# Top-16 search of the PEER score vectors moved from the up stage into the query stage of a two-block transformer kernel

## What is computed

```
q = (ht @ peer_wq).reshape(T, 8, 256)
s1 = einsum("thd,hnd->thn", q[..., :128], peer_k1)
s2 = einsum("thd,hnd->thn", q[..., 128:], peer_k2)
v1, i1 = top_k(s1, 16)
v2, i2 = top_k(s2, 16)
cand = (v1[..., :, None] + v2[..., None, :]).reshape(T, 8, 256)
sc, pos = top_k(cand, 16)
experts = take(i1, pos // 16) * 128 + take(i2, pos % 16)
gates = softmax(sc)
```

## Time and profile before

| | us |
|---|---|
| median of 3 runs | 3027.76 (3025.11 to 3029.04) |
| the profiled execution | 3026.6 |
| its span | 3024.8 |
| PE busy, share of the span | 2845.1, 94% |
| DVE busy, share of the span | 2236.1, 74% |
| ACT busy, share of the span | 1481.4, 49% |
| mean granted TensorE clock | 0.973 of 2.4 GHz |

### The profile page before, as it was taken

How to read it: one execution, slowest core, us unless ns; L and a number is a source line. 1 busy time by engine, 2 the same in 40 slices (tenths; PEclk the granted TensorE clock), 3 DMA queues, 4 the chain that set the end, 5 groups by cost and what they waited for, 6 DMA issues and landing times.

```text
span 3024.8 us, 37310 instructions
## 1 busy us (share of the span) xinstructions
PE 2845.1 (94%) x13639; PEld 2369.9 (78%) x13639; DVE 2236.1 (74%) x3019; ACT 1481.4 (49%) x1990; POOL 598.8 (20%) x480
## 2 busy tenths in 40 slices
PE   5979987999999989999999998898999999999998
PEld 3657756888888758776777788898999987888887
DVE  6465547888888853797954329999997867888886
ACT  3443235878888733544452432564665633333332
POOL 0200111111111100000000010033234434444442
PEclk7999988999999999999999998999999999999999
DMA  7544535999999833232333334587789999999995
GB/s 300 169 159 157 198 132 219 362 371 366 362 354 356 305 130 114 96 119 84 105 132 132 129 119 157 180 306 264 273 303 361 337 373 341 365 367 360 362 362 187
DMA packets 203628, 746.30 MB, mean 247 GB/s; under 512 B 24752, under 2 KB 78128, under 8 KB 146352
## 3 DMA queue, kind: packets, MB, share of 16 engines
q1 hardware_dynamic: 124656, 497.12, 45.8%
q0 software_dynamic: 56912, 179.26, 16.9%
q10 hardware_dynamic: 21872, 67.48, 5.8%
HBM read 670.80 MB, written 98.11 MB: 254 GB/s over the span
## 4 chain that ended last, share of the span: by engine, by line
PE 56%; DVE 18%; issue 5%; ACT 3%; DMA 3%; ACTq 0%; DVEq 0%; POOL 0%; SPq 0%; POOLq 0%
PE PS L550 48%; DVE wlo L1897 3%; DVE oh L2673 2%; DVE hf L2687 2%; DVE hf L2699 1%; PE PS L1151 1%; ACT whi L1227 1%; PE PS L1017 1%; PE PS L1029 1%; PE PS L856 1%; ACT HH L1867 1%; DVE zo L2422 1%; DVE sS L2726 1%; DVE i L2569 1%; DVE wkk L2572 1%
## 5 line engine op out<-in xcount | busy, mean ns | idle before, releaser
L1897 DVE TENSOR_TENSOR wlo<-raw,whi 128x2048 fp32r<-128x2048 f32 x392 | 894.7, 2289 | 351.8 <-ACT whi L1227 313.9
L1227 ACT ACTIVATE whi<-raw 128x2048 fp32r<-128x2048 f32 x392 | 750.9, 1916 | 361.2 <-PE PS L550 305.3
L550 PE MATMUL PS<-HH,whi 128*128 128x512 f32 (+1 forms) x2056 | 792.0, 385 | 47.8 <-DVE wlo L1897 24.0
L550 PE MATMUL PS<-HH,wlo 128*128 128x512 f32 (+1 forms) x2056 | 754.6, 367 | 0.0
L550 PE MATMUL PS<-HL,whi 128*128 128x512 f32 (+1 forms) x2056 | 753.3, 366 | 0.0
L550 PEld LDWEIGHTS PS<-HH,whi 128*128 128x128 f32 x2056 | 392.7, 191 | 108.6 <-DVE wlo L1897 25.4
L550 PEld LDWEIGHTS PS<-HL,whi 128*128 128x128 f32 x2056 | 392.9, 191 | 46.3 <-issue 7.7
L550 PEld LDWEIGHTS PS<-HH,wlo 128*128 128x128 f32 x2056 | 391.8, 191 | 43.1
L550 PE MATMUL PS<-whi,HH 128*128 128x512 f32 (+1 forms) x896 | 352.9, 394 | 15.9 <-DVE HL L2729 10.6
L550 PE MATMUL PS<-whi,HL 128*128 128x512 f32 (+1 forms) x896 | 348.2, 389 | 0.0
L550 PE MATMUL PS<-wlo,HH 128*128 128x512 f32 (+1 forms) x896 | 348.1, 389 | 0.0
(11 more groups left out here) (436 smaller groups left out, 3903.4 us busy)
## 6 DMA issues: line engine op xcount, KB each, us to landing
raw<-in_moe_dram SPq DMA_DIRECT2D x192, 1024.0 KB, 7.4
raw<-in_u_units_dram SPq DMA_DIRECT2D x64, 1024.0 KB
raw<-in_v_units_dram SPq DMA_DIRECT2D x64, 1024.0 KB
raw<-in_w_in_dram SPq DMA_DIRECT2D x44, 1024.0 KB
raw<-in_w_ada_dram SPq DMA_DIRECT2D x24, 1024.0 KB, 22.4
acts_dram<-sS ACTq DMA_DIRECT2D x64, 384.0 KB
gates_dram<-XT ACTq DMA_DIRECT2D x24, 1024.0 KB
sS<-acts_dram SPq DMA_DIRECT2D x42, 384.0 KB
```

The lines of the kernel that those rows point to most:

```text
L550: ins = t.matmul(dst, a, b, start=(first and n == 0), stop=(last and n == 2))
L1227: a.inc(a.e.activation(m.whi[p % HRING][:, :, :], m.raw[RAW_SLOT[load_of(p)]][:, :, :], ACT.Copy), "hi", p)
L1897: v.inc(v.e.tensor_tensor(m.wlo[h][:, :, :], m.raw[RAW_SLOT[load_of(p)]][:, :, :], m.whi[h][:, :, :].bitcast(F32), ALU.subtract), "lo_v", p)
```

## The change

1. **The search moves.** `sc` gets two halves. DVE searches vector k of all four tiles (`found(k)`, one `dve_top16` of four) straight from it in the query stage, into `v16` and `i16`, which now hold all four tiles. ACT's copy of scores k waits for `found(k-2)` in place of the DRAM store.
2. **The DRAM trip goes**: 16 stores and 4 loads on POOL's queue, with their waits, and the `s_scratch` tensor.
3. **One `whi`/`wlo` more ahead.** ACT makes `whi` of up unit 2 before its last score copy and DVE makes `wlo` of it before its last search; ACT and DVE no longer meet the others at "scored" (DVE waits there only before the first choice step).
4. **The table of the up stage.** A tile's choice has 10 steps for 13: the four searches are gone, and the two long pick steps (8200 and 6900 in the old table) are five short ones. `vector` starts at `FOUND_NS` = 13000, the margin falls from 4000 to 2000, and rows are spread evenly (120 in the up stage, 136 in the down stage). Gate steps run at most one a row.
5. Small tensors share buffers to make room, so many buffers lie at other addresses; their sizes are the same.

```diff
-CHOICE_NS = (4900,) * 4 + (1500, 4600, 0, 4600, 0, 8200, 6900, 800, 700)
+CHOICE_NS = (1500, 4600, 4600, 2000, 3400, 3400, 3400, 3400, 800, 700)
...
-LAST_GATE, LAST_ROW, UP_ROWS = 121, 126, 116
+FOUND_NS = 13000
+LAST_GATE, LAST_ROW, UP_ROWS = 119, 124, 120
...
-    tensor, vector = 0, 0
+    tensor, vector = 0, FOUND_NS
...
-        while a < CHOICE_STEPS * NT and vector < tensor + 4000:
+        while a < CHOICE_STEPS * NT and vector < tensor + 2000:
...
-                    self.sc = sb(s3, "sc", [128, 4, 128])
+                    self.sc = sb(s3, "sc", [128, 2, 4, 128])
...
         a.wait_ge("keyed", k)
-        if k:
-            a.wait_ge("score_out", k - 1)
+        if k > 1:
+            a.wait_ge("found", k - 2)
...
+    act_high(a, m, FIRST["u_units"] + HRING - 1)
     score(15)
     a.mark("scored")
-    a.wait_all("scored")
-    a.wait_ge("score_out", 15)
...
-    for n in range(8):
-        dve_low(v, m, FIRST["wq"] + n + HRING - 1)
+
+    def found(k):
+        v.wait_ge("sscore", k)
+        dve_top16(v, [(m.v16[:, i, k, :], m.i16[:, i, k, :], m.sc[:, k % 2, i, :], m.wkk[:, i, :]) for i in range(NT)])
+        v.also("found", k)
+
+    for n in range(4):
+        if n:
+            found(4 * n - 2)
+            found(4 * n - 1)
+        dve_low(v, m, FIRST["wq"] + 2 * n + HRING - 1)
+        dve_low(v, m, FIRST["wq"] + 2 * n + HRING)
+        found(4 * n)
+        found(4 * n + 1)
+    found(14)
+    dve_low(v, m, FIRST["u_units"] + HRING - 1)
+    found(15)
     v.mark("scored")
-    v.wait_all("scored")
-    v.wait_ge("score_out", 15)
...
-    for k in range(16):
-        g.wait_ge("sscore", k)
-        g.dma(e.dma_start(bass.AP(m.sd, 128 * k, [[2048, 128], [128 * 2048, 4], [1, 128]]), m.sc[:, :, :]),
-              "score_out", k)
```

More of the change, by code:

```diff
@@ L186, in peer_schedule @@
             vector += 1150
[L187 to L191, removed]
+        rows = chosen.get(0, n)
+        while 0 in chosen and c * (LAST_ROW - rows) < UP_ROWS * (n - rows) and c < UP_ROWS:
             row[2].append(c)
@@ L337, in __init__ @@
         self.mod = sb(ctx, "mod", [128, 48])
-        self.epst = sb(ctx, "epst", [128, 1])
-        self.eps2 = sb(ctx, "eps2", [128, 1])
-        self.warm = sb(ctx, "warm", [128, 1])
+        few = sb(ctx, "few", [128, 8])
+        self.epst, self.eps2, self.warm, self.ss = (few[:, a:b] for a, b in ((0, 1), (1, 2), (2, 3), (4, 8)))
         self.fn = sb(ctx, "fn", [128, 8])
@@ L2590, in dve_pair_ranks @@
     v.own(3)
-    v.inc(e.tensor_copy(quarter, m.i16[:, 0:8, :]), "pick")
+    v.inc(e.tensor_copy(quarter, m.i16[:, i, 0:8, :]), "pick")
     v.own(3)
@@ L2611, in dve_choice_step @@
     G3 = dst.rearrange("p (h k) -> p h k", h=8)
-    if r < 4:
-        v.wait_ge("scores_in", i)
-        dve_top16(v, [(m.v16[:, k, :], m.i16[:, k, :], m.sN[:, k, :], m.wkk[:, k - 4 * r, :])
-                      for k in range(4 * r, 4 * r + 4)])
-        if r == 3:
-            v.also("sn_free", i)
-    elif r == 4:
+    if r == 0:
+        if step == 0:
+            v.wait_all("scored")
         v.own()
-        v.inc(e.tensor_copy(m.i16f[:, :, :], m.i16[:, :, :]), "pick")
+        v.inc(e.tensor_copy(m.i16f[:, :, :], m.i16[:, i, :, :]), "pick")
@@ L2621, in dve_choice_step @@
         for first, n, width, o in ((0, 4, 16, 0), (4, 12, 4, 64)):
             v.inc(e.tensor_tensor(bass.AP(m.cand, o, [[1024, 128], [N_PAIR, 8], [width, n], [1, width]]),
-                                  bass.AP(m.v16, first, [[256, 128], [32, 8], [1, n], [0, width]]),
-                                  bass.AP(m.v16, 16, [[256, 128], [32, 8], [0, n], [1, width]]), ALU.add), "pick")
-    elif r in (5, 7):
-        h = 2 * (r - 5)
+                                  bass.AP(m.v16, 256 * i + first, [[1024, 128], [32, 8], [1, n], [0, width]]),
@@ new lines, in dve_choice_step @@
+    elif r == 3:
+        dve_pair_ranks(v, m, i)
+    elif r in (4, 5, 6, 7):
+        which, half = divmod(r - 4, 2)
+        ranks = bass.AP(m.wkk, 384 + 64 * half, [[512, 128], [1, 64], [0, 16]]) if which else bass.AP(
+            m.paf, 64 * half, [[128, 128], [1, 64], [0, 16]])
+        v.wait_ge("const5", "io16")
+        v.own()
+        v.inc(e.tensor_tensor(m.EQF, ranks, bass.AP(m.some, 0, [[32, 128], [0, 64], [1, 16]]), ALU.is_equal), "pick")
+        v.own()
+        v.inc(e.tensor_tensor(m.EQ, m.EQ, bass.AP(m.i16f, 128 * half + 16 * which,
+                                                  [[256, 128], [32, 4], [0, 16], [1, 16]]), ALU.mult), "pick")
+        v.own()
+        v.inc(e.tensor_reduce((m.e1, m.e2)[which][:, i, 4 * half:4 * half + 4, :], m.EQ, AX.X, ALU.add), "pick")
+    elif r == 8:
@@ L2653, in dve_choice_step @@
                               ALU.subtract), "gsub", i)
-    elif r == 12:
+    elif r == 9:
         v.wait_ge("gexp5", i)
@@ L3034, in pool_peer @@
     for n in range(128):
-        for step in PEER[n][0]:
-            i, r = choice_of(step)
-            if step == 0 or r == 4 and step + CHOICE_STEPS < NT * CHOICE_STEPS:
-                if step:
-                    g.wait_ge("sn_free", i)
-                    i = choice_of(step + CHOICE_STEPS)[0]
-                g.dma(e.dma_start(m.sN[:, :, :].rearrange("p k n -> p (k n)"),
-                                  m.sd[128 * i:128 * i + 128, :, :].rearrange("t k n -> t (k n)")), "scores_in", i)
         for step in PEER[n][2]:
```

60 lines of the change are left out of this document (22 added, 38 removed).

## The result

The changed kernel takes 2982.68 us (median of 4 runs, 2978.2 to 2987.42); the kernel before took 3026.44 beside it (4 runs, 3023.0 to 3029.04). The ratio is 0.9856, 95% interval 0.9838 to 0.9875. I had forecast 2992 with a range of 2984 to 3006.

A forecast was written before the change was run, and what follows sets the result against it. DVE was taken to bound the first two thirds of the up stage, PE the rest. Up stage 36 us less, query stage, DRAM trip, down stage and addresses 0: 3026.6 becomes 2991, median 2992, range 2984 to 3006.

The forecast's parts named there:

- The search in the query stage: Query stage: 16 searches at 5.34 us cost DVE 85 us, the lag stays inside PE's room; priced at 0.
- DRAM trip, unit 2, unit 3: Start of up stage: the 23.7 us score wait and PE's 9.9 us stop go; both units' `wlo` come in time.
- DVE's chain up to the `wlo` of unit 30: Up stage to row 57: 277 us of DVE work plus 7 of waits after 1811.6, done at 2095.6 us.
- PE starts row 60 there: Up stage: PE starts row 60 at 2095.6, has 334.6 us left, ends at 2430.2 for 2466.0: 36 us less.
- the floor of 624.8: Up stage if PE never waited: 624.8 us against 672.8, so 48 us at most; rival chance 0.07, 2979.
- The down stage ... 0 by the rows: Down stage: four fewer gathered rows worth 0, at most 4 us of PE idleness; its start may move a few us.
- The price of the rows by their bytes: Down stage bound by bytes: four rows, 2.1 MB, take 5.8 us, gain 42 instead of 36; rival 2986, chance 0.08.
- Addresses: Whole kernel: other buffer addresses add or resize no instruction; 0, give or take 3 us.
- The base: Starting time: profiled execution of 3026.6 us becomes 2991; the median of runs lies 1.2 us above it.
- near 2430: End of the up stage: gelu 127 near 2430 us as a sign of being right; later than 2445 wrong.
- the search overruns: Query stage: PE stops from about 5.7 us a search, gain gone at 7.6, 3043 at 8.5; chance 0.03.
- The DVE bound for longer: Up stage: waits at 14 and 7 us more for gate chains, gain 22, time 3005; rival, chance 0.17.

The follow-up runs named there:

- the layout alone: Kernel before with only the change's packing and order of small buffers ahead of the PEER layer: ratio 0.9985 to the kernel before, median 3019.2 us.
- The doubled search: Changed kernel with each of the 16 query-stage searches made twice: 3067.56 us, ratio 1.0144 to the kernel before.
- The run with the late exponential: Changed kernel with ACT's softmax exponential four rows and DVE's finish five rows behind the pick, gate steps starting later: median 2973.78 us, ratio 0.9833.
- the one with slower rows: Late-exponential kernel with gathered rows due at 0.6 a row until the fourth tile's choice is made, faster after: median 2967.94 us, ratio 0.9815.
- the faster version: Changed kernel with late exponential, slower gathered rows and 128 rows gathered in the up stage: median 2964.74 us, ratio 0.9804 to the kernel before.
- with the table: Kernel before with only the change's table rules, 120 rows gathered in the up stage, searches and DRAM trip left in place: ratio 0.9957.
- with the last due rows put back: Changed kernel with LAST_GATE 121 and LAST_ROW 126 for 119 and 124, still 120 rows: median 2983.8 us, ratio 0.9868 to the kernel before.

## Why the prediction was wrong, step by step

- **The search in the query stage: right.** Counted from the last `qT2` copy, which came 9.2 us earlier than in the profile before, the last search should end at 1802.4 us; it ended at 1802.5. ACT's copies wait 9.5 us for searches in seven waits, the longest 3.0, and PE never stops for them; the stage is 0.3 us longer, as it is with the layout alone. One search takes 5.42 us start to start where I had taken 5.34:

```profile
1726.59 0.87 DVE L2573 MAX8 v<-sc 128x8 f32<-128x128 f32 x4 [0.45 <-ACT sc L1755]
...
1732.01 0.88 DVE L2573 MAX8 v<-sc 128x8 f32<-128x128 f32 x4
```

- **DRAM trip, unit 2, unit 3: right.** No wait for scores, no stop for a `wlo`.
- **DVE's chain up to the `wlo` of unit 30: right.** 284 us forecast from the last search, 281.4 measured (1802.5 to 2083.9), with the 28 `wlo`, 41 gate steps and 41 rows that I had counted and 6.4 us of waits, where I had 7 and three of 1.7 for the exponentials. The doubled search confirms that it is one chain.
- **"PE starts row 60 there": wrong, 11.9 us.** This is the step of the up stage that failed. I let PE be held by `wlo` alone, so that it could run ahead of DVE's row 57 by the ring's depth. When that `wlo` was done, at 2083.9, PE had finished only row 58's matmuls and stood in its gate product, and it began row 60 at 2095.8. What held it was ACT's exponential, behind a DVE that came 8.8 us late: 6.3 of the 11.9 us are this stop and 1.3 the slower row 59 after it, and the other 4.3 remain, for which the earlier stops (9.11 and 1.80 us) are the likely cause. I had read that wait the other way only, DVE 1.72 us for ACT, and had allowed 7 us on DVE's side for gate waits where they had to be counted on PE's. From row 60 on the price was good: 332.7 us against 334.6. The shorter chain and these last rows gave back 4.5 us, so the stage missed by 7.4. The run with the late exponential takes back 11.4 us, and the one with slower rows ends at 629.3, near the floor of 624.8 that I had worked out from the earlier trace rows.
- **"The down stage ... 0 by the rows": wrong, 10.6 us, and the miss that put the time below the range.** The miss of the up stage worked the other way. I had read PE's 406 of 410 us from the earlier trace rows, a window that begins 74 us behind the start of the stage, and had written that the start "may move a few us either way" without looking at it. The rows before it show PE at 54.0 us of 60 with a clock of 0.95: 8.7 us lost that could be won, and 5.9 were. Most of the rest are the four gathered rows: 3.3 to 3.8 us in the kernel before (against the layout run and against before), 6.4 for eight in the changed kernel. PE's 4 us of idleness in that window, my "at most", was about what the rows were worth.
- **The price of the rows by their bytes: half right.** My estimate by bytes, from the 362 GB/s of the earlier trace rows, was 5.8 us for four rows, or 1.45 each; the sum took 0, and the runs say 3.8 at most. A row cost 0.83 to 0.95 us between 116 and 120 rows in the kernel before, 0.80 between 112 and 120 in the changed one, and 0.45 between 120 and 128 in the faster version, where PE was busy 399.3 of 400 us. So at a DMA share of 1.00 with PE at 99% neither set the pace alone. The Trainium skill (SBUF - State Buffer, "A bandwidth-pool intuition that's wrong (but worth ruling out)") says that HBM is almost always the end-to-end bottleneck; this stage agrees with it only in part, at 0.45 to 0.95 us a row.
- **Addresses: 0, give or take 3 us.** The layout alone took 2 to 7 us off.
- **The base.** The median of three runs shown was 3027.76; over later runs it is 3022.8 to 3024.8. I started some 3 us high.

The parts close: -28.4, +0.3 and -10.6 from the stages make -38.7, in which a part of the layout's effect is contained; the 2 us that came off ahead of the first `qT2` with the layout make it 41. (They are from one profile each, where that mark varies by more.) The measured difference is 40 to 42 against the later medians and 44 in the first comparison. From the forecast of 2992, +8 for the up stage, -11 for the down stage, -2 for the layout and -3 to -5 for the base give 2982 to 2984. My forecast was right about the one large term, too good by 8 us on what PE would make of it, and short on two terms that I had set to nothing: misses of opposite sign, of which the larger won. It is luck, too, that gelu 127 came at 2428.5 where I had written "near 2430": the part ahead of the query stage was 9.6 us shorter in this profile, and without that it would have stood at 2438. Of the rivals, the slower one (the search overruns) is a real mechanism that only needs a larger search: at twice the price the kernel was 1.4% slower than before, and the 84.7 us more are about what its rule gives, 16 times the added price. The DVE bound for longer, 3005, was the up stage's direction but not its size.

Open: how much of the 26 us is the wait for the scores from DRAM (the 9.9 us stop) and how much the 85 us of search taken out of the rows, which no run separates; what makes the part before the query stage vary by 10 us between executions, why the layout helps, and which rule of the table took away the third stop at the start of the down stage.

## What to carry to other kernels

In a kernel whose engines each run a fixed order, a lag of one is passed on at every place where another asks for its result, not only at the large buffer between them. For each wait on the lagging engine ask what stands behind it on the waiting one; four small steps, placed in the row of their producer, cost about 11 us here beside the 26 that the moved work won. Put such a step later by about as many rows as the lag is long; four rows were enough here, and other distances weren't tried. And a stage priced at nothing must be priced in its first microseconds too: a window that starts after the seam hides both what is lost there and what a change will win.

## What the runs showed of the hardware

- A stop can cost PE more than its own length. In the 100 us from 1841 us on, with stops of 9.11 and 1.13 us, PE was busy 89.8 us at a clock of 0.95, so about 85.3 us at full clock were done and 14.7 lost. But the clock does not follow from the idleness alone: in the first 60 us of the down stage the same amount of it (2.8 to 2.9 us) stood beside a clock of 1.00, 0.97 or 0.94 in three kernels (after, with the table, with the last due rows put back), and the difference of 3.5 us between the ends was larger than the idleness.
- DVE ran at 93 of 104 us busy in the query stage, with MAX8, FIND_INDEX8 and MATCH_REPLACE8 on 128x128 tiles just copied by ACT, and PE's stage took 87.3 us with these searches and without them (layout run). Four vectors' top 16 took 5.42 us start to start here; the repeated search of the doubling run took 5.35.
- The time at which the same instructions reach the same place, 1700 us into the kernel, varied over the 14 profiles of these kernels by 10 us (1695.4 to 1705.5), 0.3% of the whole. Stage lengths behind that place repeated within 0.2 us in two profiles of the changed kernel. So here a profile's stages told effects that the medians of four or five runs could not.
